# The first block's softmax attention: the reciprocal of the row sum as a diagonal from ScalarE, multiplied in by TensorE

## The reference

```
def fox_attention(q, k, v, log_f, key_valid):
    ...
        s = jnp.einsum('bhqd,bhkd->bhqk', q[:, :, start:end], k[:, :, :end]).astype(jnp.float32) * scale
        s = s + cum[:, :, start:end, None] - cum[:, :, None, :end]
        ...
        p = jax.nn.softmax(jnp.where(allowed, s, -jnp.inf), axis=-1)
        outs.append(jnp.einsum('bhqk,bhkd->bhqd', p.astype(v.dtype), v[:, :, :end]))
```

## Time and profile before

| | |
|---|---|
| median of 3 runs | 2567.19 us |
| lowest and highest | 2565.28, 2571.98 us |
| the profiled execution's own time | 2574.36 us |
| its span, first to last instruction | 2573.0 us |
| its mean granted TensorE clock | 0.967 |
| PE busy | 2448.4 us, 95% |
| DVE busy | 1676.7 us, 65% |
| ACT busy | 1246.6 us, 48% |
| products of L825 | 96 |

### The profile page before, as it was taken

How to read it: one execution, slowest core, us unless ns; L and a number is a source line. 1 busy time by engine, 2 the same in 40 slices (tenths; PEclk the granted TensorE clock), 3 DMA queues, 4 the chain that set the end, 5 groups by cost and what they waited for, 6 DMA issues and landing times.

```text
span 2573.0 us, 45875 instructions
## 1 busy us (share of the span) xinstructions
PE 2448.4 (95%) x18769; PEld 2322.9 (90%) x18769; DVE 1676.7 (65%) x3006; ACT 1246.6 (48%) x2099; POOL 33.6 (1%) x63
## 2 busy tenths in 40 slices
PE   7999999999999989999999998999999999769999
PEld 6999788899999977899999998989998999457999
DVE  5656777776575487778648846756656765455664
ACT  5444455554354445556445634645445644334542
POOL 2000000000000000000000000000000000000000
PEclk9999999999999999999999998989999999677999
DMA  7655433565465453346655653427655665412653
GB/s 193 174 179 141 117 91 109 141 182 176 148 178 175 158 132 99 99 137 189 189 183 162 183 176 102 119 58 191 185 184 157 180 189 171 127 41 83 180 181 140
DMA packets 589729, 385.85 MB, mean 150 GB/s; under 512 B 44587, under 2 KB 564111, under 8 KB 589392
## 3 DMA queue, kind: packets, MB, share of 16 engines
q1 hardware_dynamic: 585408, 374.00, 50.5%
q10 hardware_dynamic: 2336, 5.92, 0.6%
q0 software_dynamic: 1776, 2.98, 0.4%
HBM read 378.59 MB, written 4.19 MB: 149 GB/s over the span
## 4 chain that ended last, share of the span: by engine, by line
PE 87%; DVE 8%; ACT 2%; issue 1%; DMA 1%; ACTq 0%; DVEq 0%
PE bank L516 86%; DVE wlo L1906 2%; DVE ry L1925 1%; DVE ry L1923 1%; PE bank L825 0%; ACT whi L1243 0%; DVE smh L2357 0%; DVE rst L1927 0%; PE bank L601 0%; ACT rst L1264 0%; DMA xs<-in_x 0%; PE bank L1163 0%; ACT rst L1266 0%; DMA wraw<-in_w_ffn_gu 0%; DVE ssb L2677 0%
## 5 line engine op out<-in xcount | busy, mean ns | idle before, releaser
L1906 DVE TENSOR_TENSOR wlo<-wraw,whi 128x1024 fp32r<-128x1024 f32 (+2 forms) x723 | 866.7, 1205 | 290.7 <-ACT whi L1243 287.3
L1243 ACT ACTIVATE whi<-wraw 128x1024 fp32r<-128x1024 f32 (+2 forms) x723 | 746.9, 1042 | 596.5 <-DMA wraw<-in_w_ffn_gu 175.2
L516 PE MATMUL bank<-xhi,whi 128*128 128x256 f32 (+2 forms) x4024 | 606.6, 291 | 40.7 <-ACT xhi L1279 24.6
L516 PE MATMUL bank<-xhi,wlo 128*128 128x256 f32 (+2 forms) x4024 | 592.8, 287 | 11.4 <-DVE wlo L1906 11.4
L516 PEld LDWEIGHTS bank<-xhi,whi 128*128 128x128 f32 (+1 forms) x4024 | 535.4, 190 | 63.0 <-ACT xhi L1279 27.1
L516 PE MATMUL bank<-xlo,whi 128*128 128x256 f32 (+2 forms) x4024 | 581.4, 285 | 0.0
L516 PEld LDWEIGHTS bank<-xhi,wlo 128*128 128x128 f32 (+1 forms) x4024 | 535.5, 190 | 15.4 <-DVE wlo L1906 15.1
L516 PEld LDWEIGHTS bank<-xlo,whi 128*128 128x128 f32 (+1 forms) x4024 | 528.2, 188 | 0.2
L516 PE MATMUL bank<-act_hi,wlo 128*128 128x256 f32 (+1 forms) x1408 | 400.5, 284 | 0.0
L516 PE MATMUL bank<-act_lo,whi 128*128 128x256 f32 (+1 forms) x1408 | 400.1, 284 | 0.0
L516 PE MATMUL bank<-act_hi,whi 128*128 128x256 f32 (+1 forms) x1408 | 399.1, 283 | 0.0
(11 more groups left out here) (396 smaller groups left out, 1815.9 us busy)
## 6 DMA issues: line engine op xcount, KB each, us to landing
wraw<-in_w_ffn_gu SPq DMA_DIRECT2D x176, 512.0 KB, 3.9
wraw<-in_w_ffn_down SPq DMA_DIRECT2D x88, 512.0 KB, 3.2
wraw<-in_ffn_w_gate SPq DMA_DIRECT2D x88, 512.0 KB, 3.9
wraw<-in_ffn_w_up SPq DMA_DIRECT2D x88, 512.0 KB, 3.9
wraw<-in_ffn_w_down SPq DMA_DIRECT2D x88, 512.0 KB, 3.3
wraw<-in_w_in SPq DMA_DIRECT2D x80, 512.0 KB, 3.9
wraw<-in_a_w_in SPq DMA_DIRECT2D x24, 384.0 KB, 3.2
wraw<-in_w_out SPq DMA_DIRECT2D x16, 512.0 KB, 3.8
```

The lines of the kernel that those rows point to most:

```text
L516: return E.matmul(out_, lhsT, rhs, start=first, stop=last, skip_group_check=True)
L1243: A.activation(flat(whi, u), flat(wraw, u), ACT.Copy).then_inc(S("hi"), 1)
L1906: V.tensor_tensor(flat(wlo, u), flat(wraw, u), flat(whi, u).bitcast(F32), ALU.subtract).then_inc(lo_ready[u % RING], 1)
```

## The change

A unit's probabilities are no longer multiplied by the reciprocal on DVE. DVE only forms the reciprocal (semaphore `fox_r` in place of `fox_p`). ACT then scales the identity by it, row by row, into one of two 128 x 128 pieces of `ssum` (`fox_dg`, semaphore `fox_d`). PE forms an ordinary fp32 product of the unscaled block with that diagonal, where it transposed with the identity: the result is the transposed block with each query's column scaled. DVE's wait for `fox_p` ahead of the mask goes too. The diff shows the helper, then PE's part, then ACT's, which stands ahead of the copy of unit i - 2, then DVE's.

```
+    def fox_dg(i):
+
+        return ssum[:, P * (i % 2):P * (i % 2) + P]
...
-                        E.wait_ge(S("fox_p"), g + 1)
+                        E.wait_ge(S("fox_d"), g + 1)
                         E.wait_ge(S("tv_c"), c.tv)
                         if g > 0:
                             E.wait_ge(S("fox_c"), g)
                         for st, (s0, ns) in enumerate(TOK_TILES1[:tl + 1]):
-                            m = E.transpose(bank[3][0:ns, st * P:st * P + n], pp1[(i - 2) % 3][0:n, s0:s0 + ns], ident[0:n, 0:n])
+                            m = mm(bank[3][0:ns, st * P:st * P + n], pp1[(i - 2) % 3][0:n, s0:s0 + ns], fox_dg(i - 2)[0:n, 0:n], True, True)
...
+                    if 0 <= i - 1 < FOX_N:
+                        pair, tl, t0, n, h, hh, W = units[i - 1]
+                        z = (i - 1) % 2
+                        A.wait_ge(S("fox_r"), FOX_N * L + i)
+                        if i - 1 >= 2:
+                            A.wait_ge(S("fox_t"), FOX_N * L + i - 2)
+                        A.activation(fox_dg(i - 1)[0:n, 0:n], ident[0:n, 0:n], ACT.Copy, scale=stat_a[0:n, 4 * z + 3:4 * z + 4]).then_inc(S("fox_d"), 1)
...
-                        pp = pp1[(i - 1) % 3][0:n, 0:W]
                         V.wait_ge(S("fox_e"), g + 1)
-                        own(V.reciprocal(rd, den))
-                        wait_own()
-                        V.tensor_scalar(pp, pp, rd, None, ALU.mult).then_inc(S("fox_p"), 1)
+                        V.reciprocal(rd, den).then_inc(S("fox_r"), 1)
...
-                        if i >= 2:
-                            V.wait_ge(S("fox_p"), g - 1)
```

## The result

The change makes the kernel slower: median 2586.28 us (2583.62 to 2590.9, 5 runs) against 2571.43 us of before beside it (2565.28 to 2574.29, 5 runs); ratio 1.0065, 95% interval 1.0046 to 1.0083. A second set of five (e6) gave 1.0065 again, 1.0052 to 1.0077. By the ratio that is 16.7 us, where 9.7 were forecast, and 2586.28 lies above the range's 2584. Two executions are left out throughout because they took far longer than all others: the profiled one of e3 (8158 us) and one of e4 (3941 us).

What follows compares the result with a forecast made beforehand. PE, 95% busy, was taken to bound the kernel, with DVE work in fox covered. Added records +9.6 us and a later copy +0.1 made +9.7 on the median 2567.19: 2576.9 us, 0.38% slower, range 2570.5 to 2584.

Steps and rivals of the forecast that it cites:

- the range's 2584: Whole kernel: upper end of the forecast range, 2570.5 to 2584 us, including two rivals and scatter between medians.
- a term of 0.1 in all: Last turn with values: copy 0.26 us later, PE 0.21 later itself; 0.05 us per layer, 0.1 in all.
- 0.26 within ends of 0 and 0.51: ACT: price of one diagonal in us, from a 128 x 128 copy; upper end the wide exp; 12.6 us over 48 units.
- the late diagonal: Rival, turns with gla's output: ACT makes the diagonal late, 8 x 0.5 = 4 us on top, 2580.9 us; chance 0.05.
- DVE's gift: Rival, not slower: shorter DVE chain ends the drain's wait, 6.6 us gained, 2560.6 if products cost nothing; chance 0.06.
- four times the transpose: Rival, PE's slots in fox: product costs each slot four times over, 39 us added, 2606 us; chance 0.03.
- the price of the added records: PE in fox: 96 transposes become products with two records each; +9.6 us, between estimates of 10.7 and 9.0.
- my upper end: PE in fox: added record costs the transpose's whole slot again; 0.21 + 0.37 + 0.24 = 0.82 us, times 16: +13.1 us.
- the span that I had written down for it: Profile after: start-to-start times of 0.33 to 0.36 us (one wide), 0.58 to 0.62 (two wide), 0.43 to 0.55 (three narrow).
- The price of 0.064 us a record: PE, narrow records: from sixteen of 16 columns with 128 columns of weights in 1.02 us; 0.192 for three added.
- The pairs that I had first: PE in fox: transpose against following product with values, differences 0.15, 0.21, 0.31 us; sum 0.67, times 16: +10.7 us.
- the worse row: PE: second pricing, added records only, from rows of sixteen records at 0.124 and 0.064 us each; +9.0 us.

Runs made afterwards that it cites:

- e6: The change itself, unaltered, timed again against the kernel before in a second set of five runs; ratio 1.0065 (1.0052 to 1.0077).
- e3: Kernel before, with ACT also forming the 48 diagonals, which nothing reads, ahead of its copy from bank 3; ratio 0.9995 (0.9983 to 1.0007).
- e4: The change, but units with 16 query rows keep multiplication and transposes, their diagonals formed and unread; ratio 1.0044 (1.0027 to 1.0061).
- e1: Kernel before, with fox's transposes made fp32 products with the identity; DVE and ACT keep their work; ratio 1.0058 (1.0042 to 1.0074), 14.9 us.
- e2: Kernel before, without DVE's multiplication by the reciprocal, output not normalised, transposes kept; ratio 1.0003 (0.9991 to 1.0015).
- e12: Kernel before, with gla's products of qz with kz issued by half of the rows (heads 0, 2, 1, 3); executed once, no ratio.
- e13: Kernel before, with 48 more parameter transposes in the first feed-forward part, 3.2 us added on PE, fox untouched; ratio 1.0035 (1.0023 to 1.0047).
- e7: The change, with probabilities and diagonal as fp32r, one record per product; ratio 0.9985 (0.9976 to 0.9995), 3.9 us faster than the kernel before.
- e9: Kernel before, with only the 128-query-row units' transposes made products with the identity, no diagonals; ratio 1.0034 (1.0022 to 1.0047).
- e14: Kernel before, with 96 more parameter transposes in the first feed-forward part, 6.5 us added on PE; ratio 1.0030 (1.0020 to 1.0041).
- e15: Kernel before, with 48 more transposes of memory rows behind the last fox, 5.2 us added on PE; ratio 1.0022 (1.0012 to 1.0033).
- e8: The change, with 128 moving columns in place of 16 in the 16-query-row units' products; executed once, no ratio; three products 0.95 us against 0.68.

## Why the prediction was wrong

**Right.** PE bounds fox, and its groups lengthen the turn one for one (13.1 us of slots against 13.2 of stretch; in e1 one wait covers 0.5 us of them). DVE's multiplication is worth nothing (e2). The diagonal hides on ACT (e3) and was ready 4.7 us ahead. Where it does show, at the last turn with values, it is as forecast: it delays the copy, PE is late itself, and the wait goes from 0.54 to 0.55 us, against a term of 0.1 in all; the 0.5 us between the change and e1 are this same delay without that cover. It takes 0.39 us, where I took 0.26 within ends of 0 and 0.51; with its cover there that cost nothing. The rivals of the late diagonal and of DVE's gift did not occur, nor did that of four times the transpose. By the Trainium skill (TensorE: Matmul & The Clock Gate, Terms) the transpose mode is 4 times faster for FP32; the trace does not bear that out as time: the slots here are 1.5, 1.8 and 2.8 times longer.

**The step that failed first: the price of the added records.** I took 9.6 us; it was 13.1 by the slots. That this is also my upper end is luck: its terms were 0.21, 0.37 and 0.24 us, the measured ones 0.10, 0.28 and 0.44, and only the sums agree at 0.82. None of the three slots lies in the span that I had written down for it (0.33 to 0.36, 0.58 to 0.62, 0.43 to 0.55; measured 0.31, 0.65, 0.69). The one wide unit was over-priced, 0.10 instead of 0.124; the two wide under-priced, 0.28 instead of 0.248; the error is the narrow one, 0.44 us instead of 0.192, which alone is 16 x 0.25 = 4.0 us. It has three parts. The price of 0.064 us a record came from sixteen records of gla that alternate between the two halves of the rows; e12 shows that they owe 0.027 us a record to that order, and 0.091 is the price without it: 0.08 us for three added records. The rest to 0.114, another 0.07, on 16 rows of weights and at the head of a group, no run separates. And I left the transposes' own slot as it was, but the other three records are a product's too, at 0.114 us and not at the transposes' 0.083: 0.09 us, which I had put at nothing. The pairs that I had first, with the product by the values in the same place, gave 0.31 for this unit and 10.7 us in all, and I moved away from them towards the worse row. Their products load 64 columns of weights and not 128; whether that is their difference to 0.44 was not tried.

**The second: what lies outside fox.** I had no term for it. By the ratio the change costs 16.7 us, 3.5 more than its fox; by the medians, 14.9, it is 1.7 more. Every timed kernel in which two records take the place of one shows 2 to 5 us of this kind by its ratio, and e13 has 5.8 without any; e7 has the reverse, 5.2 us less than its fox. Taken alone it is weak: of these kernels none has its fox more than 1.2 us below its interval, and for the change's first set, e1 and e9 the fox lies inside it; e13 stands 2.7 us clear. The clock is where profiles of the same work differ. The stretch from 1715 to 1775 us (end of the second block's mixer), granted clock behind the five engines' busy times, in after and then in e1:

```profile
1715.00:1775.00 60.00, 55.02 (x373) 50.81 (x373) 34.27 (x68) 28.45 (x52) 0.00 (x0) 0.86 0.43 113
```

```profile
1715.00:1775.00 60.00, 54.97 (x414) 51.48 (x413) 36.68 (x71) 31.95 (x55) 0.00 (x0) 0.94 0.44 108
```

The products of `cellp_hi` there span 33.8 us in after and 34.1 in before, but 28.1 in e1, e7 and e12, with equal work; the longer ones have a part of it at 1.2 GHz. So these 6 us do not tell the change from before, and they are nearly all of the 6.2 us that e7's profile has less behind fox. Whether a kernel meets such stretches more often in its executions, which would be the 3.5 us, I cannot show: a profile sees one execution. A shift in time alone was not seen to set it (e14, e15). This stays open.

**The base.** The forecast stood on the median of three runs, 2567.19. Two runs more put it at 2571.43. On that base the same +9.7 us would have been 2581.1, and the range's upper end 2588.2, above the measured time. The miss of 9.4 us is 4.2 of base, 3.4 of price (13.1 less 9.7) and 1.8 outside fox, by the medians.

## What to carry to other kernels

Where TensorE bounds, an fp32 transpose is not free to replace by a product: it leaves one record where the product leaves two, and here 96 of them cost 13 us for 14 us of VectorE time that nobody waited for. Price an added product from a row with the same rows of the array, the same columns of weights and the same place in the turn; a cheaper row of the same shape can owe a part of its price to its neighbours' order. Price all records of the product, and not only the added ones. And compare a stretch that repeats to a tenth of a microsecond with the timed ratio: what is left over is a question of its own, and here it stays one.

## What the runs showed of the hardware that was not expected

- Sixteen fp32 records with 64 rows of weights take 1.02 us when they alternate in pairs of products between the halves of the array's rows, and 1.46 us grouped by half; with 128 moving columns 1.19 and 1.64 (e12).
- An fp32 product with 16 rows and 128 columns of weights takes 0.114 us a record with 16 moving columns and 0.158 with 128 (e8), 0.40 ns a column.
- In fp32r one record takes the place of two. A single product with the diagonal then takes 0.35 us to the next group and two take 0.37, but the single one starts 0.34 us after the scores, where it was 0.54 (e7).
- A copy with a column operand as scale takes 0.39 us for 128 x 128 from SBUF, and the next instruction of ACT starts 0.29 us after its start; a plain copy from PSUM takes 0.26 (after).
- 3.2 us of PE work, placed early, cost 9.0 us (5.9 to 12.1), and 6.5 us in the same place 7.7 (5.1 to 10.5), by the ratios (e13, e14).
